# Gated delta rule in a three-block layer: norms through transposes and per-row columns, a last inversion round on 64-blocks, keys of two heads transposed twice

## What is computed

```python
q = q * lax.rsqrt(jnp.sum(q * q, axis=-1, keepdims=True) + EPS) * (GDN_HEAD_K ** -0.5)
k = k * lax.rsqrt(jnp.sum(k * k, axis=-1, keepdims=True) + EPS)
...
amat = jnp.where(strict, kk * decay * beta, 0.0)
t = lax.linalg.triangular_solve(eye + amat, rhs, left_side=True, lower=True, unit_diagonal=True)
u, w = t[..., :GDN_HEAD_V], t[..., GDN_HEAD_V:]
v_new = u - w @ state
o = (q * exp(gc)) @ state + (qk * decay) @ v_new
state = state * exp(gc_last) + (k * exp(gc_last - gc)).T @ v_new
...
o = o * lax.rsqrt(jnp.mean(o * o, axis=-1, keepdims=True) + EPS) * norm_w
o = o * jax.nn.silu(z)
```

## Time and profile before

| | |
|---|---|
| median of 3 runs | 3248.73 us (3247.9 to 3250.78) |
| the profiled execution's own time | 3243.82 us |
| its span | 3241.5 us |
| TensorE busy | 3089.1 us, 95% |
| VectorE, GpSimd, ScalarE busy | 1693.4, 1186.7, 1071.9 us |
| mean granted TensorE clock | 0.973 of full |
| the delta rule's stretch | 254 to 782 us of the span |

### The profile page before, as it was taken

How to read it: one execution, slowest core, us unless ns; L and a number is a source line. 1 busy time by engine, 2 the same in 40 slices (tenths; PEclk the granted TensorE clock), 3 DMA queues, 4 the chain that set the end, 5 groups by cost and what they waited for, 6 DMA issues and landing times.

```text
span 3241.5 us, 39147 instructions
## 1 busy us (share of the span) xinstructions
PE 3089.1 (95%) x15912; PEld 2519.6 (78%) x15912; DVE 1693.4 (52%) x3287; ACT 1071.9 (33%) x1725; POOL 1186.7 (37%) x564
## 2 busy tenths in 40 slices
PE   7989999999999998999999979999979999899999
PEld 5768888887888886867877758888767777688887
DVE  6866657456577516556775363331166666633310
ACT  4442323233322223222323433222235454332221
POOL 3442333233444442213313334444433333444443
PEclk9998999999999999989999989999989999999999
DMA  3211212112344431002011213323222212223232
GB/s 127 80 48 33 66 40 66 53 43 82 104 144 148 132 102 56 21 27 72 27 33 59 91 33 98 98 98 98 85 86 66 69 59 70 70 91 98 98 104 85
DMA packets 72339, 247.80 MB, mean 76 GB/s; under 512 B 8160, under 2 KB 8544, under 8 KB 72032
## 3 DMA queue, kind: packets, MB, share of 16 engines
q1 hardware_dynamic: 72160, 245.30, 23.5%
HBM read 243.18 MB, written 2.10 MB: 76 GB/s over the span
## 4 chain that ended last, share of the span: by engine, by line
PE 84%; DVE 11%; ACT 2%; issue 1%; POOL 1%; DMA 0%; SPq 0%; DVEq 0%; ACTq 0%; POOLq 0%
PE bank L927 22%; PE bank L929 22%; PE bank L928 22%; PE bank L967 5%; PE bank L961 2%; PE bank L938 1%; PE bank L945 1%; PE bank L1387 1%; PE bank L1405 1%; PE bank L1227 1%; PE bank L1396 1%; POOL t L2774 1%; PE bank L1275 1%; DVE u L1575 0%; DVE sm L1476 0%
## 5 line engine op out<-in xcount | busy, mean ns | idle before, releaser
L2741 POOL TENSOR_TENSOR R<-W,R 128x1024 fp32r<-128x1024 f32 (+2 forms) x454 | 1050.8, 2319 | 1839.1 <-ACT R L2354 1839.1
L927 PE MATMUL bank<-u,R 128*128 128x512 f32 (+1 forms) x3440 | 1395.7, 406 | 27.6 <-issue 7.3
L929 PE MATMUL bank<-u,R 128*128 128x512 f32 (+1 forms) x3440 | 1353.5, 393 | 0.0
L928 PE MATMUL bank<-u,R 128*128 128x512 f32 (+1 forms) x3440 | 1352.9, 393 | 0.0
L927 PEld LDWEIGHTS bank<-u,R 128*128 128x128 f32 (+1 forms) x3440 | 653.0, 190 | 190.6 <-issue 29.1
L929 PEld LDWEIGHTS bank<-u,R 128*128 128x128 f32 (+1 forms) x3440 | 651.9, 190 | 143.7 <-issue 1.0
L928 PEld LDWEIGHTS bank<-u,R 128*128 128x128 f32 (+1 forms) x3440 | 653.9, 190 | 129.9 <-issue 5.0
L2354 ACT ACTIVATE R<-W 128x1024 fp32r<-128x1024 f32 (+2 forms) x454 | 451.9, 1001 | 137.0 <-PE bank L929 127.2
L967 PE MATMUL bank<-t,t 128*128 128x128 f32 x1552 | 196.6, 277 | 3.4 <-DVE t L1767 1.9
L967 PEld LDWEIGHTS bank<-t,t 128*128 128x128 f32 x1552 | 187.2, 192 | 9.6 <-DVE t L1767 2.6
L2384 ACT ACTIVATE u<-t 128x512 fp32r<-128x512 f32 x126 | 78.5, 630 | 323.4 <-DVE t L1597 246.2
(11 more groups left out here) (375 smaller groups left out, 2878.5 us busy)
## 6 DMA issues: line engine op xcount, KB each, us to landing
W<-in_in SPq DMA_DIRECT2D x48, 512.0 KB, 3.6
W<-in_ff_in SPq DMA_DIRECT2D x44, 512.0 KB, 4.0
W<-in_g_qkv SPq DMA_DIRECT2D x24, 512.0 KB, 3.6
W<-in_ada SPq DMA_DIRECT2D x24, 512.0 KB, 3.7
W<-in_f1g SPq DMA_DIRECT2D x22, 512.0 KB, 3.6
W<-in_f1u SPq DMA_DIRECT2D x22, 512.0 KB, 3.7
W<-in_f2g SPq DMA_DIRECT2D x22, 512.0 KB, 3.6
W<-in_f2u SPq DMA_DIRECT2D x22, 512.0 KB, 3.6
```

Source lines behind the costliest of these rows:

```text
L927: e.matmul(b[0:cols, :], wh, hi, start=(k == 0), stop=False)
L928: e.matmul(b[0:cols, :], wh, lo, start=False, stop=False)
L929: i = e.matmul(b[0:cols, :], wl, hi, start=False, stop=(k == KT - 1))
L2741: e.tensor_tensor(R[q % NH][:, 1024:1024 + n], W[p % NW][:, 0:n], R[q % NH][:, 0:n].bitcast(F32), SUB).then_inc(*PN.pool.up("lo", key))
```

## The change

- Norms of q and k: T transposes k and q first (`hq`, now a TensorE step), S squares them out of PSUM (`hqs`), V sums along the free axis (two `tensor_reduce`), does the Newton steps on 8 columns and multiplies k's transpose by its column (`hn`). T transposes that back (`hnp`), S copies it out as the normed k (`hn2`). q stays unnormed; its factor goes into the output's norm. The `token_sum` and `spread` of both are gone.
- `hk` takes the transposed k that `hn` left in tile `KT_[h]`. For heads 4 and 5 this tile is one that the inversion overwrites, so k is transposed there again (`AGAIN`). Heads 6 and 7 keep it in tiles that `p_ssm` must have left.
- Output: `hs3` swaps stationary and moving operand, so the output has tokens on partitions; S squares each chunk with an accumulated sum (`ho` per chunk); V makes the factor, multiplies and T transposes back (`hon`, `hos`); V multiplies by weight and gate in one instruction (`ho2`).
- Round n = 2 of the delta rule's inversions: each matmul is 64 stationary columns by 64 moving columns over 64 rows (`corner`); V touches 64 partitions by 256 elements; G's mask and its wait are left out.
- Head `h = 1` starts after `hu` of head 0; costs and predecessors in the planner's tables follow the new steps, so the whole list between the first head and the last is written anew: 4377 steps in all before, 4385 now. The list ahead of it and behind it is the same.

```diff
-    hq="s1.23", hqp="p1.78", hn="v2.9", hnp="p.95", hn2="v1.4",
+    hq="p.87", hqs="s1.23", hn="v6.2", hnp="p.44", hn2="s.6",
-    ho="s1.21", hop="p.89", hon="v2.7", hos="p.47", ho2="v1.43",
+    ho="s.47", hon="v4.9", hos="p.44", ho2="v.85",
...
-    "hq": lambda h: [("conv2", "qkv", 3 * h + 1)] + ([("ho2", h - 2)] if h >= 2 else []),
+    "hq": lambda h: [("conv2", "qkv", 3 * h + 1)] + ([("ho2", h - 2)] if h >= 2 else [("hu", 0)] * h),
...
+            def corner(b, l, x, k):
+                for m in range(4):
+                    s = m * 128
+                    i = e.matmul(b[0:64, s + 64:s + 128], l[k:k + 64, s:s + 64], x[k:k + 64, s + 64:s + 128], start=True, stop=True)
+                return i
...
-                quad(bank[V_.bz], t(V_.d), t(V_.p)).then_inc(*IV.pe.up("y", v, n))
+                i = corner(bank[V_.bz], t(V_.L), t(V_.p), 64) if n == 2 else quad(bank[V_.bz], t(V_.d), t(V_.p))
...
-            def hqp(h):
-                token_sum(bank[q.X], t(q.d), 1, True, False)
-                token_sum(bank[q.X][:, 4:8], t(q.e), 1, False, True).then_inc(*GD.pe.up("sum", h))
+            def hq(h):
+                w.wait_ge(*(GD.dve.at("o", h - 2) if h >= 2 else SS.dve.at("y", 7)))
+                w.wait_ge(*CV.dve.at("out", "qkv", 3 * h + 1))
+                if h == 0:
+                    w.wait_ge(*SS.dve.at("yn", 7))
+                transpose4(bank[q.Y], t(q.k)).then_inc(*GD.pe.up("kt", h))
+                transpose4(bank[q.Z], t(q.q)).then_inc(*GD.pe.up("qt", h))
             def hnp(h):
-                spread(bank[q.Y], parts[q.nw][:, 0:4], parts[q.nw][:, 8:12]).then_inc(*GD.pe.up("rq", h))
-                spread(bank[q.Z], parts[q.nw][:, 4:8], parts[q.nw][:, 12:16]).then_inc(*GD.pe.up("rk", h))
+                transpose4(bank[q.Z], t(KT_[h])).then_inc(*GD.pe.up("kn", h))
             def hk(h):
-                transpose4(bank[q.Z], t(q.k)).then_inc(*GD.pe.up("kt", h))
+                if h in AGAIN:
+                    transpose4(bank[q.Z], t(q.k)).then_inc(*GD.pe.up("k2", h))
...
-                i = e.matmul(bank[q.Z][:, s], vn, t(q.dec)[:, s], start=True, stop=(c == 0))
+                i = e.matmul(bank[q.Z][:, s], t(q.dec)[:, s], vn, start=True, stop=(c == 0))
...
-                token_sum(bank[q.X], t(q.d), 1, True, True).then_inc(*GD.pe.up("osum", h))
...
-                spread(bank[q.Y], parts[q.nw][:, 0:4], parts[q.nw][:, 4:8]).then_inc(*GD.pe.up("ro", h))
+                transpose4(bank[q.Y], t(q.d)).then_inc(*GD.pe.up("on", h))
...
+                e.tensor_reduce(n[:, 0:4], v3(t(q.e)), AX.X, ADD).then_inc(*GD.dve.up())
+                e.tensor_reduce(n[:, 4:8], v3(t(q.d)), AX.X, ADD).then_inc(*GD.dve.up())
+                newton(GD.dve, n[:, 0:8], n[:, 8:16], n[:, 16:24], n[:, 24:32])
+                e.tensor_tensor(v3(t(KT_[h])), v3(bank[q.Y]), n[:, 16:20].unsqueeze(2).broadcast_to([128, 4, 128]), MUL)
...
-                e.tensor_tensor(v3(t(q.d)), v3(bank[q.Z]), kcols(K_END)[...], MUL).then_inc(*GD.dve.up("kd", h))
+                e.tensor_tensor(v3(t(KT_[h])), v3(bank[q.Z] if h in AGAIN else t(KT_[h])), kcols(K_END)[...], MUL)
...
+                newton(GD.dve, n[:, 0:4], n[:, 4:8], n[:, 8:12], n[:, 12:16])
+                e.tensor_tensor(v3(t(q.d)), v3(bank[q.Z]), n[:, 8:12].unsqueeze(2).broadcast_to([128, 4, 128]), MUL)
+                e.scalar_tensor_tensor(out=o, in0=bank[q.Y], scalar=P("gdn_norm_w"), in1=t(q.e), op0=MUL, op1=MUL)
...
-                e.activation(t(YG[h]), bank[q.Z], ACT.Copy).then_inc(*GD.act.up("o", h))
-                e.activation(t(q.d), t(YG[h]), ACT.Square).then_inc(*GD.act.up("sqo", h))
+                e.activation(t(q.kb)[:, 384:512], bank[q.Z][:, c * 128:c * 128 + 128], ACT.Square,
+                             accum_out=small[q.nw][:, c:c + 1]).then_inc(*GD.act.up("sqo", h, c))
```

More of the change, by code:

```diff
@@ L145, with upper @@
     max = match_replace = memset = dma_start = then_inc = it
+def upper(ap):
+    return ap[0:64, :].rearrange("p (t i) -> p t i", t=4)[:, :, 64:128]
 def v3(ap):
@@ L491, in inversion @@
     for n in range(levels):
-        out += [("im", n) + v] + ([("iu", n - 1) + v] if n else []) + ([("iq", n + 1) + v] if n + 1 < levels else []) + [("in_", n) + v]
+        out += [("im", n) + v] + ([("iu", n - 1) + v] if n else []) + ([("iq", n + 1) + v] if n + 1 < min(levels, 2) else []) + [("in_", n) + v]
     return out
 def gdn_head(h):
-    out = [("hq", h), ("hqp", h), ("hn", h), ("hnp", h), ("hn2", h), ("hg", h), ("hb", h), ("hu", h)]
+    out = [("hq", h), ("hqs", h), ("hg", h), ("hn", h), ("hnp", h), ("hn2", h), ("hb", h), ("hu", h)]
     out += inversion(("g", h), 3) + [("hk", h)]
     for c in range(4):
-        out += ([("hs1", h, c)] if c else []) + [("hs2", h, c), ("hs3", h, c)]
-    return out + [("ho", h), ("hop", h), ("hon", h), tiles("g_z", h, ("hz", h)), ("hos", h), ("ho2", h)]
+        out += ([("hs1", h, c)] if c else []) + [("hs2", h, c), ("hs3", h, c), ("ho", h, c)]
+    return out + [("hon", h), tiles("g_z", h, ("hz", h)), ("hos", h), ("ho2", h)]
 def rwkv_pair(p):
@@ L1782, in im @@
                 w.wait_ge(*IV.pe.at("y", v, n))
+                if n == 2:
+                    e.tensor_copy(upper(t(V_.e)), upper(bank[V_.bz])).then_inc(*IV.dve.up("y", v, n))
+                    return
                 e.tensor_copy(t(V_.e), bank[V_.bz]).then_inc(*IV.dve.up("y", v, n))
@@ L1884, in ho2 @@
                 o = t(YG[h])
-                w.wait_ge(*GD.pe.at("ro", h))
-                w.wait_ge(*GD.act.at("sqo", h))
-                e.scalar_tensor_tensor(out=o, in0=o, scalar=P("gdn_norm_w"), in1=bank[q.Y], op0=MUL,
-                                       op1=MUL).then_inc(*GD.dve.up())
-                w.wait_ge(*GD.dve.now())
-                e.scalar_tensor_tensor(out=o, in0=o, scalar=0.5, in1=t(q.e), op0=MUL, op1=MUL).then_inc(*GD.dve.up("y", h))
+                w.wait_ge(*GD.pe.at("on", h))
+                w.wait_ge(*GD.dve.at("got", "g_z", h))
+                if h >= 4:
+                    w.wait_ge(*PN.pe.at("dense", "p_ssm", 7))
+                e.scalar_tensor_tensor(out=o, in0=bank[q.Y], scalar=P("gdn_norm_w"), in1=t(q.e), op0=MUL,
+                                       op1=MUL).then_inc(*GD.dve.up("y", h))
                 GD.dve.when["o", h] = GD.dve.n
```

140 lines of the change are left out of this document (76 added, 64 removed).

## The result

| | before | after |
|---|---|---|
| median (4 runs each) | 3248.32 us (3247.36 to 3250.78) | 3228.53 us (3227.64 to 3229.93) |
| ratio, 95% interval | | 0.9939 (0.9927 to 0.9951) |
| profiled execution, span | 3243.82, 3241.5 us | 3228.13, 3226.3 us |
| mean granted clock | 0.973 | 0.971 |

A forecast was written before the change was run, and what follows sets the result against it. The prediction took TensorE's issued work to bound the kernel. Its terms, -37.7 - 4.3 - 0.5 + 8.7 + 1.0 = -32.8 us on 3243.8, gave 3211.0; with the median 4.9 us higher, 3216 us, range 3203 to 3235.

The forecast's parts named there:

- the likeliest case: Whole kernel: the forecast's own case, 3209 to 3227 us, given a chance of 0.68.
- TensorE's records: Delta rule: column sums and spreads go, corners get cheaper, transposes are added; net 37.7 us less.
- I take 0.055, the same shape but for the rows: Inversion corners: each 64 by 64 matmul priced at 0.055 us instead of 0.111, saving 7.2 us (0 to 9).
- The start: Start of head 0: TensorE idle 4.4 us, then half clock; cost 7.7 us instead of 12.0, 4.3 us less.
- the cheaper of the two ends: Start of head 0: low end of the half-clock loss, 2.3 us of 2.3 to 4.4, clock back after 4.6 us.
- Waits inside: Inside the delta-rule stretch: 2.5 us of Newton waits go, 2 us of new waits come; net 0.5 us less.
- both have a projection tile or more ahead of them in the new order: Transposed k before hnp and scaled output before hos: called covered, with 2 us (0 to 6) allowed for waits.
- VectorE costed at nothing: Delta rule: VectorE's added and removed instructions about even and hidden under TensorE, with VectorE idle for 220 us.
- the six multiplies by the end decay: Delta rule: now reading both inputs from SBUF, they may collide with GpSimd; at most 3 us, put into the range.
- The end of head 7: Last chunks and output norm lose cover: TensorE idle 12.4 us instead of 3.7, so 8.7 us more.
- VectorE's queue at some heads: Rival: norms queued on VectorE delay evacuations at three or four of 8 heads; 3231 to 3236 us, chance 0.16.
- against it: Argument against the rival of VectorE's queue: VectorE's idle share and the small waits before.

The follow-up runs named there:

- short splits: GpSimd's instruction of each weight split in the delta-rule stretch cut to 8 columns: 3238.1 us in the kernel before, 3206.7 us in the changed kernel.
- start_after: Changed kernel with eight pieces of g_qkv 2 and 10 moved ahead of the three waits before head 0: 3222.3 us, 0.9921 of the kernel before.

## Why the prediction was right or wrong

The time lay in the range and the direction was right; the size was not, and the likeliest case, 3209 to 3227, missed by 1.5 us.

- **TensorE's records, 37.7 less.** Right but for the corners. Between the two kernels with short splits, sums and spreads drop by some 45 us of TensorE's time (41.9 predicted; 32 of the sums stood at half clock), transposes rise by 11.6 (11.4), corners save 5.4 (7.2). The step "I take 0.055, the same shape but for the rows" used the distance inside a row of four records; a call of eight pays 0.17 us more (0.61 less 8 x 0.055), at its first record and at its last, which the price of a lone group did not hold.
- **The start.** Idle 4.15 us for 4.4. The clock was back at 259, under 4 us after the transposes, so the cheaper of the two ends was right.
- **Waits inside.** The step that failed: "both have a projection tile or more ahead of them in the new order; I allow 2 us (0 to 6)". It was 13.1, where the kernel before has 4.5. The cover was there, but it was counted against a Newton chain of 3.9 us, and the chain was up to 6.4 us longer where splits ran; only 6.3 of it stand at the two steps of that sentence, the rest at others.
- **VectorE costed at nothing.** The same error from the other side. I weighed GpSimd against the six multiplies by the end decay, the only instructions whose inputs the change moved to SBUF, and bounded them at 3 us; two of the six do stand (1.27 and 2.34 us, the others 0.69). I did not put the question to the 256 small Newton instructions, which had read SBUF all along. Their busy time in the stretch, summed over the groups that read and write `sm`, is 53.3 us before (216 of them) and 81.8 after; with short splits 39.8 and 48.6. So collisions took 13.5 us of VectorE before and 33.2 after. The number of small instructions hardly changed: with those that write `sr` it is 248 before, and 11 of them take more than 0.6 us; after it is 257, and 23 do, though GpSimd is busy for less of the stretch (159.7 us for 171.2). So the new order puts the chains beside more splits; no run changes that alone, and why the planner's list falls out so stays open. The Trainium skill (SBUF — State Buffer, Who interferes with whom) says that instructions with two inputs in SBUF contend with GpSimd's reads, that `tensor_scalar` can contend in a two-port mode, and that the blocked one waits for the whole instruction. The traces agree on the first kind: L1489 stood 2.30 us. A `TENSOR_SCALAR` stood too, 2.32 us in start_after; whether it ran in that mode no trace tells.
- **The end of head 7, 8.7 more.** Idle 9.3 us for 12.4: chunks 2.7 for 4.1, norm 6.6 for 8.3. The Newton chain took 3.2 us, not 3.9: the 3.9 was read at the same head before, where one of its instructions had itself stood beside a split (VectorE, GpSimd, kernel before):

```profile
774.13 1.10 DVE L1488 TENSOR_SCALAR sm<-sm 128x4 f32<-128x4 f32 x1
773.90 1.30 POOL L2741 TENSOR_TENSOR R<-W,R 128x512 fp32r<-128x512 f32 x1 [4.88 <-ACT R L2354]
```

So a collision was in the very price: the earlier trace rows show only the lines ahead of it and behind it. At half clock TensorE's own work fills more of every hop (its four transposes 1.1 us). Right was that nothing covers the norm; that it stood behind `hz` on VectorE I had in the sum but not seen as the cause.
- **Rivals.** VectorE's queue at some heads (3231 to 3236, 0.16) was nearest in size and place, wrong in mechanism: with the queue as it is and GpSimd out of the way 0.9 of the 13.1 us of waits are left. The point "against it", VectorE's idle share, was no argument, as an average says nothing of a chain of dependent instructions.
- **Behind the stretch** I counted nothing; R gave back 3.0; the granted clock took 4.7 more (44.9 us of busy time lost there before, 49.6 after, summed in the same way), and idle time was a little less.

## What to carry to other kernels

A chain of small dependent VectorE instructions that read SBUF costs its own time plus one GpSimd instruction for each that meets one; before a wait is called covered, lay GpSimd's instructions beside the chain in the time line, for the old instructions as for the new. A change may be worth its whole TensorE work only once the other engines' collisions are cleared: here the same edit gave 19.6 us in the stretch as it was and 30.9 with GpSimd out of the way. And judge a stage by two marks inside the trace, one ahead of it and one behind, not by the total: the clock behind it moved totals by 12 us, and the same work ahead of it ended up to 4.4 us apart.

## What the runs showed of the hardware

- A subtraction of 128x1024 from SBUF to SBUF takes GpSimd 2.4 us and VectorE some 1.2; moving 54 of them made VectorE busier and the changed kernel 20 us faster.
- A small VectorE instruction (0.17 us alone) beside a GpSimd split lasts until the split ends. In the row of three splits in the kernel after, one small VectorE instruction gets in between each two: 2.35, 2.31 and 2.30 us beside 7.09 us of splits.
- Small matmuls of 64x64 cost 0.077 us a record over a call of eight, against 0.11 for 128x128: a quarter of the work saves 30%.
- The same TensorE work ran at full clock in some kernels and at half clock for 27 us in others: 48 records over 64 rows took 17.94 and 25.42 us.
